# Even and odd heads paired at every second tick in four attention sets of a two-layer trunk

## What is computed

```
# fox: causal, with a decay c from the forget gates
s = einsum('bqhd,bkhd->bhqk', q, k) * scale + (c[..q] - c[..k]);  s = where(causal, s, NEG_INF)
o = einsum('bhqk,bkhd->bqhd', softmax(s), v)
# dilated, for (window, dilation) = (128,1), (512,4), (2048,16):
o_g, lse_g = softmax attention inside the band, by residue class of the dilation
o = sum_g softmax_g(lse)[g] * o_g
x = x + o @ w_out;   x = x + square(relu(rmsnorm(x) @ w1)) @ w2
```

## Time and profile before

| what | us |
|---|---|
| median of 3 runs | 1559.63 (1558.02 to 1560.07) |
| the profiled execution | 1556.66 |
| its span in the profile | 1554.9 |
| F0, from its first scores to those of F1 | 104.38 |
| F1, to the first transposes of the output projection's second half | 68.90 |
| G4, from its first scores to those of the next step | 96.22 |
| G7, as F1 | 56.93 |

### The profile page before, as it was taken

The page is one execution under the profiler, slowest core; times in us unless marked ns, Lnnn a source line. Parts: engine busy times, 40 slices in busy tenths (PEclk is TensorE's granted clock), DMA queues, the critical chain, the costliest instruction groups (busy, mean ns, idle before and its releaser), DMA issues.

```text
span 1554.9 us, 24762 instructions
## 1 busy us (share of the span) xinstructions
PE 1527.7 (98%) x9284; PEld 1229.9 (79%) x9284; DVE 938.8 (60%) x1658; ACT 704.3 (45%) x1192; POOL 381.9 (25%) x515
## 2 busy tenths in 40 slices
PE   7999999999999999899999999999999999999999
PEld 6777666878888888788878877887877888888887
DVE  4457644547474758645647586655645566565778
ACT  5433344355454545445434344444353453535353
POOL 3301100020111511162427254334711110101010
PEclk9999999999999999999999999999999999999999
DMA  5221110557565656333222322222224466675753
GB/s 167 81 68 55 42 54 2 162 138 186 135 152 154 139 166 119 125 101 87 69 82 83 124 68 69 82 69 83 72 94 137 126 144 189 125 199 108 196 120 90
DMA packets 111600, 173.57 MB, mean 112 GB/s; under 512 B 12688, under 2 KB 45456, under 8 KB 111504
## 3 DMA queue, kind: packets, MB, share of 16 engines
q1 hardware_dynamic: 91904, 134.51, 27.7%
q0 software_dynamic: 17408, 33.56, 13.3%
q10 hardware_dynamic: 2192, 4.20, 0.8%
HBM read 165.89 MB, written 6.36 MB: 111 GB/s over the span
## 4 chain that ended last, share of the span: by engine, by line
PE 88%; DVE 5%; POOL 4%; issue 2%; ACT 1%; DMA 0%; DVEq 0%; POOLq 0%; ACTq 0%
PE ps L620 57%; PE ps L935 18%; PE ps L745 3%; PE ps L691 3%; PE ps L719 3%; PE ps L757 2%; PE ps L659 1%; POOL qrs L1820 1%; PE ps L683 1%; DVE w_l L1320 1%; DVE w_l L1605 1%; DVE x_sb L1665 1%; ACT p_sb L1085 1%; ACT w_h L1008 1%; POOL e_all L1868 0%
## 5 line engine op out<-in xcount | busy, mean ns | idle before, releaser
L620 PE MATMUL ps<-w_h,act_h 128*128 128x512 f32 x768 | 311.2, 405 | 6.8 <-DVE w_l L1320 3.4
L620 PE MATMUL ps<-w_h,act_l 128*128 128x512 f32 x768 | 303.4, 395 | 0.0
L620 PE MATMUL ps<-w_l,act_h 128*128 128x512 f32 x768 | 303.1, 395 | 0.0
L1320 DVE SCALAR_TENSOR_TENSOR w_l<-w_raw,gain_t,w_h 128x512 fp32r<-128x512 f32 x188 | 142.3, 799 | 104.7 <-ACT w_h L1008 104.6
L620 PE MATMUL ps<-act_h,w_h 128*128 128x512 f32 x512 | 200.0, 391 | 2.0 <-DVE w_l L1578 2.0
L620 PE MATMUL ps<-act_h,w_l 128*128 128x512 f32 x512 | 199.5, 390 | 0.0
L620 PE MATMUL ps<-act_l,w_h 128*128 128x512 f32 x512 | 199.4, 389 | 0.0
L1820 POOL TENSOR_TENSOR qrs<-qss,m_half 128x8 f32<-128x8 f32 x64 | 110.4, 1725 | 316.6 <-DVE qss L1366 316.0
L1085 ACT ACTIVATE p_sb<-ps,negmax 128x128 f32<-128x128 f32 (+4 forms) x256 | 88.1, 407 | 209.2 <-DVE negmax L1421 114.3
L620 PEld LDWEIGHTS ps<-w_h,act_h 128*128 128x128 f32 x768 | 152.9, 199 | 36.7 <-issue 9.1
L620 PEld LDWEIGHTS ps<-w_l,act_h 128*128 128x128 f32 x768 | 152.7, 199 | 28.5
(11 more groups left out here) (223 smaller groups left out, 2431.9 us busy)
## 6 DMA issues: line engine op xcount, KB each, us to landing
w_raw<-in_dil_w_in SPq DMA_DIRECT2D x72, 512.0 KB, 3.7
raw<-in_mlp_w SPq DMA_DIRECT2D x64, 512.0 KB, 4.8
raw<-in_mlp_w POOLq DMA_DIRECT2D x48, 512.0 KB, 5.7
w_raw<-in_mlp_w SPq DMA_DIRECT2D x32, 512.0 KB, 4.9
w_raw<-in_fox_w_in SPq DMA_DIRECT2D x22, 512.0 KB, 3.7
p_sb<-in_mlp_w SPq DMA_DIRECT2D x16, 512.0 KB, 5.4
pT_sb<-in_mlp_w SPq DMA_DIRECT2D x16, 512.0 KB, 6.2
w_raw<-in_mlp_w POOLq DMA_DIRECT2D x16, 512.0 KB, 7.0
```

The costliest lines, as they stand in the source:

```text
L620: return mm(ps_out, lhs[i], rhs[j], start=(k == 0 and term == 0), stop=(k == KT - 1 and term == 2))
L1320: last = v.scalar_tensor_tensor(w_l[u % WR][:, j, :], raw(u)[:, j, :], gain_t[:, norm, k:k + 1], f(w_h[u % WR][:, j, :]), ALU.mult, ALU.su ...
```

## The change

In sets 0, 1, 4 and 7 (`paired`), TensorE does attention work at even ticks alone: the scores of a pair as before, then the transposes of both ticks a-2 and a-1, then the values of both ticks a-4 and a-3, one after the other. At odd ticks it does dense products alone. The output of a tick on VectorE and its merge on GpSimd come one tick later (`values_lag` 4 in place of 3). The value products of an even and an odd head get separate slots of the PSUM bank `o_ps`. The output of both waits until the values of the whole pair are done, and the values of a pair wait until both outputs of the pair before are done. `normalise` moves behind `output`. `turn_qk` is put at an even tick where that tick has none yet. In F1 and G7 the fills stand behind the values, and `FILL_TICKS` is shifted. The number of products, transposes and vector operations is the same.

```
+def paired(s):
+    return SETS[s][0] in ("fox", 0)
+def values_lag(s):
+    return 4 if paired(s) else 3
...
+    if paired(attend):
+        taken = set()
+        for i in reversed(range(len(due))):
+            c, s, b = due[i]
+            if (c + c % 2) not in taken:
+                due[i] = (c + c % 2, s, b)
+            taken.add(due[i][0])
+    return [(s, b) for c, s, b in due if c == a]
...
-FILL_TICKS = {1: [7, 9, 11, 13, 15, 17, 19, 21, 23, 24, 25, 26], 7: [5, 7, 9, 10, 11, 12, 13, 14, 15, 16, 17, 18]}
+FILL_TICKS = {1: [8, 10, 12, 14, 16, 18, 20, 22, 23, 24, 25, 26], 7: [6, 7, 8, 9, 10, 12, 13, 14, 15, 16, 17, 18]}
...
-                    pe.wait_ge(o_done, a)
+                    pe.wait_ge(o_done, a - a % 2 if paired(s) else a)
...
+                    slot = 2 * (a % 2) + slot if paired(s) else q
...
-                        if 2 <= a <= nt + 1:
-                            turn_probs(attend, t0 + a - 2)
+                        if not paired(attend):
+                            if 2 <= a <= nt + 1:
+                                turn_probs(attend, t0 + a - 2)
+                            if 3 <= a <= nt + 2:
+                                values(attend, t0 + a - 3)
+                        elif a % 2 == 0:
+                            for odd in range(2):
+                                if 2 <= a <= nt:
+                                    turn_probs(attend, t0 + a - 2 + odd)
+                            for odd in range(2):
+                                if 4 <= a <= nt + 2:
+                                    values(attend, t0 + a - 4 + odd)
                         if proj is None:
                             out_terms(attend, a)
-                        if 3 <= a <= nt + 2:
-                            values(attend, t0 + a - 3)
...
-                dve.wait_ge(pv_done, a + 1)
+                dve.wait_ge(pv_done, a - a % 2 + 2 if paired(s) else a + 1)
...
-                        if 4 <= a and SETS[attend][0] == 0 and tl[a - 4][2]:
-                            normalise(attend, tl[a - 4][0])
-                        if 3 <= a <= nt + 2:
-                            output(attend, t0 + a - 3)
+                        lag = values_lag(attend)
+                        if lag <= a < nt + lag:
+                            output(attend, t0 + a - lag)
+                        if SETS[attend][0] == 0:
+                            for b in range(max(a - lag - 1, 0), nt if a == n - 1 else a - lag):
+                                if tl[b][2]:
+                                    normalise(attend, tl[b][0])
```

More of the change, by code:

```diff
@@ L171, in turns_of_tick @@
         return []
-    return [(s, b - 1) for s, b in banks_of_tick(proj, attend, a - 1) if 1 <= b <= QK_SET]
+    due = [(c + 1, s, b - 1) for c in range(ticks_of_step(attend))
+           for s, b in banks_of_tick(proj, attend, c) if 1 <= b <= QK_SET]
+    if paired(attend):
[6 more added lines that the diff above has]
+    return [(s, b) for c, s, b in due if c == a]
 def new_slot(s, h):
@@ L740, in values @@
                 c = 0
-                for q, k0, nk in SCORE_BANKS[SETS[s][0]][i]:
+                for slot, (q, k0, nk) in enumerate(SCORE_BANKS[SETS[s][0]][i]):
+                    slot = 2 * (a % 2) + slot if paired(s) else q
                     for k in range(nk):
@@ L744, in values @@
                             rows = slice(side * P // 2, (side + 1) * P // 2)
-                            last = mm(o_ps[rows, q, 0:VC], pT_sb[:, a % 2, c * P + rows.start:c * P + rows.stop],
+                            last = mm(o_ps[rows, slot, 0:VC], pT_sb[:, a % 2, c * P + rows.start:c * P + rows.stop],
                                       v_sb[s % 2][:, k0 + k, h // 2, head_cols(h)], start=(k == 0), stop=(k == nk - 1))
@@ L1476, in output @@
                 n = len(tiles)
-                dve.wait_ge(pv_done, a + 1)
+                slots = slice(2 * (a % 2), 2 * (a % 2) + n)
+                dve.wait_ge(pv_done, a - a % 2 + 2 if paired(s) else a + 1)
                 if kind == "fox":
-                    link(v.reciprocal(rden[:, 0, span], o_ps[:, span, own_one(h)]))
-                    v.tensor_tensor(o_sb[:, span, (HS * half + h) // 2, value_cols(h)], o_ps[:, span, own_values(h)],
-                                    rden[:, 0, span].unsqueeze(2).broadcast_to([P, n, HD]), ALU.mult).then_inc(o_done, 1)
+                    link(v.reciprocal(rden[:, 0, slots], o_ps[:, slots, own_one(h)]))
+                    v.tensor_tensor(o_sb[:, span, (HS * half + h) // 2, value_cols(h)], o_ps[:, slots, own_values(h)],
+                                    rden[:, 0, slots].unsqueeze(2).broadcast_to([P, n, HD]), ALU.mult).then_inc(o_done, 1)
                 elif kind == 1:
@@ L1492, in output @@
                         dve.wait_ge(merged, m - 1)
-                    v.tensor_copy(o_ring[:, m % 2, span, 0:VC], o_ps[:, span, 0:VC]).then_inc(o_done, 1)
+                    where = slots if paired(s) else span
+                    v.tensor_copy(o_ring[:, m % 2, span, 0:VC], o_ps[:, where, 0:VC]).then_inc(o_done, 1)
             def normalise(s, h):
@@ L1500, in normalise @@
                 o = o_sb[:, :, (HS * half + h) // 2, head_cols(h)]
-                link(v.reciprocal(rden[:, 1, :], o[:, :, own_one(h)]))
-                v.tensor_tensor(o[:, :, own_values(h)], o[:, :, own_values(h)], rden[:, 1, :].unsqueeze(2).broadcast_to([P, NT, HD]), ALU.mult).then_inc(normed, 1)
+                link(v.reciprocal(rden[:, h % 2, :], o[:, :, own_one(h)]))
+                v.tensor_tensor(o[:, :, own_values(h)], o[:, :, own_values(h)], rden[:, h % 2, :].unsqueeze(2).broadcast_to([P, NT, HD]), ALU.mult).then_inc(normed, 1)
             def step(proj, attend):
@@ L1855, in step @@
                 for a in range(n):
-                    if attend is not None and 3 <= a <= len(ticks_of(attend)) + 2:
-                        merge(attend, TICK0[attend] + a - 3)
+                    lag = values_lag(attend) if attend is not None else 0
+                    if attend is not None and lag <= a < len(ticks_of(attend)) + lag:
+                        merge(attend, TICK0[attend] + a - lag)
                     for s, b in banks_of_tick(proj, attend, a):
```

## The result

| | before | after |
|---|---|---|
| median of 11 runs each, side by side | 1559.5 (1557.17 to 1560.45) | 1562.39 (1561.57 to 1563.22) |
| the profiled execution | 1556.66 | 1562.33 |
| its span | 1554.9 | 1560.3 |

The ratio is 1.0022, with a 95% interval from 1.0014 to 1.003: the changed kernel is slower by 2.9 us. The prediction was 1562.3. The ratios of e9 to e11 further down leave out one run of the kernel before that took 2159.85 us at a mean granted clock of 0.655.

What follows compares the result with a forecast made beforehand. TensorE was taken as the bound, almost level in F1 and G7 with a chain through VectorE's output. F0 -2.3, G4 -2.1, F1 +5.4 and G7 +1.7 gave +2.7, median 1562.3 us; range 1554 to 1568, its own 1559 to 1565.5.

Runs made afterwards that it cites:

- e9: e8 with `normalise` put one tick later; median 1544.7 us, 0.9917 of the kernel before.
- e11: e9 with `turn_qk` put back at the ticks where the kernel before has it; median 1546.8 us, 0.9929 of the kernel before.
- e2: The change in sets 1 and 7 (F1 and G7) alone, the others in the order of the kernel before; median 1566.1 us, ratio 1.0048 to before.
- e12: The kernel before, unchanged, profiled a second time; 1559.4 us (one run), span 1557.4.
- e8: Changed kernel, odd head's maximum ahead of the output in all four sets, twelve unused dense products in G7's last wait; 1547.2 us, 0.9924 of the kernel before.

## What to carry to other kernels

Joining small products on the array pays a fixed amount a group, but the wait for the joined result moves too: look at what stands behind that wait on the next in-order engine, and move it ahead in the same edit. A wait at the end of a chain is no slack for what is late within the chain: in G7 it stayed at 3.0. Take a profile of the kernel before twice, and compare stretches of the program rather than whole spans, before a difference of a few us is charged to an edit. A predicted saving is worth its number only in a stretch where the engine has no wait that can swallow it.

## What the runs showed of the hardware

The granted clock fell to half (the 1.2 GHz level) for a few us behind idle times of TensorE: 3.0 us at the end of G7, 1.6 and 2.7 us between the layers, and in F1 of e2 behind two waits of 1.3 and 1.5. Dense products then start 0.43 apart (643.19 to 643.62) in place of 0.23. Where it can be read off by itself, a stretch costs 1.0 to 1.6 us. What had not been expected is that the same idle time has this effect in one execution and not in another: behind the end of G7 it was there in e12 and not in the first profile of the same kernel, with the same work and the same wait ahead of it. Of the 14 profiles 10 have it between the layers, and one in F1, though after has the same two waits in F1. What decides it is open. The Trainium skill (TensorE: Matmul & The Clock Gate, What's actually happening) has the low clock as the resting state which activity lifts; the traces agree so far that it follows idle time, and that none of the three profiles with products in the wait of G7 has it behind G7 (e8, e9, e11), against 8 of 11 without.
